# A head norm with one product and no spread, a quarter's end in another order, and one more early weight tile in a one-core fp32 block pair

## The chip, the cores and the metric

One of the eight cores of a Trainium2 chip runs the whole program. The metric is device time in microseconds (us), lower is better. The kernel before takes 2919.57 us, the median of 3 runs that lie between 2918.3 and 2920.6 us. In the text, PE is TensorE, DVE is VectorE, ACT is ScalarE, POOL is GpSimd and SP is the engine that issues most transfers.

## The reference, cut to what matters

The program computes two transformer-like blocks after one another on 1024 tokens of width 1024, in float32. The first block has a mixer with a recurrence (heads of 64 channels) and a convolutional feed-forward; the second puts 16 meta tokens in front (1040 columns), has a gated linear recurrence (8 heads, 128 keys, 64 values) beside a pooling mixer, and a feed-forward. Three places matter here: two norms per head of 64 channels, and the projection of the second block's mixer.

```
# block 1, after the recurrence: norm per head (64 channels)
mu = mean(y, -1); var = mean(square(y - mu), -1)
y = (y - mu) * rsqrt(var + GN_EPS)           # then gain, bonus, gate
# block 2, mixer
z = rmsnorm(h, norm1_g)
proj = z @ w_in                              # 1024 x 5632, 44 column blocks of 128
q, fl, iv, og, pin, ga, gb = split(proj)
S_t = diag(f_t) S_{t-1} + (1 - f_t) i_t^T ;  o_t = S_t^T q_t
o = o * rsqrt(mean(o * o, -1) + EPS)         # per head of 64 channels
o = o * head_g * silu(og)
```

## The kernel before, in words

Engines run own instruction streams that wait for each other by semaphores. Features lie on the 128 partitions and tokens along the row. A large float32 product is done as three products of a high and a low part: ACT copies a raw weight tile (128x1024) to its high part, POOL subtracts to get the low part, and PE multiplies hi by hi, hi by lo and lo by hi.

**Stages.** Three groups of stages stand behind one another, with a barrier of all engines between them (`clear_semaphores`): norm, projections and recurrence of block 1; then `middle`, with block 1's output projection, its feed-forward and block 2's mixer; then `ending`, with the branch products, block 2's output projection and feed-forward. The middle group's last instruction on any engine therefore holds up the next group on all of them.

**The recurrence's quarters** (`recurrence1`). The tokens are worked in four quarters of 256. While quarter i is prepared, the chain of the quarter before runs between. All small PE results go through a ring of two PSUM banks, `rec_e`, in the order of `quarter_pieces`: a piece may start when the piece two before it has been emptied. At the end of a quarter PE computes the score pieces `lk0` to `lk3` (emptied by DVE, `key_scores`) and the turned pieces `vt0`, `vt1`, `bt0`, `bt1` (emptied by ACT, `turns_out`), and the `var` piece, the sum of squares for the norm of the quarter before, which ACT turns into a standard deviation (`result_std`). DVE in between also forms the quarter's keys (`removal_key`, `undecayed_removal`, `undecayed_key`) and the reciprocal of that deviation (`result_inverse`).

**The join of feed-forward and mixer.** At the end of block 1's feed-forward the token tiles 0 to 7 and the 16 meta tokens pass one after another through: last product (PE), addition (DVE), statistics (ACT), scale, residual and norm (DVE), turn by 8 transposes (PE, `turn_tile`), high part (ACT), low part (DVE). `turn_tile(n)` turns token tile n-1; so `turn_tile(8)` is the last, with token tile 7. Into the gaps the mixer's first weight tile is placed: `first_dense` is piece 0 (400 columns, 24 products), `second_dense` half of piece 1, `rest_of_second` the other half.

**The mixer** (`mixer2`). Its projection has 44 blocks of three pieces (`dense`), 348, 348 and 344 columns. A piece is 24 products. All go through a ring of three PSUM banks, `mix_e`, in the order of `mixer_pieces`, mostly emptied by ACT. After the first nine blocks come 32 slots, four to a head. A slot holds three pieces and the recurrence of 256 tokens of one head: DVE builds the tree of decays for the next slot (`forget`, `double`, `whole_tiles`) and masks the scores (`mask`), PE makes `scores`, `outputs`, `keys`. After each pair of heads (8 slots) comes the norm: ACT squares the pair's output (`squares`), PE sums over each head into 16 rows (`sums_of`: 8 products of 130 columns with a `window` of ones), ACT takes the root, DVE the reciprocal of an 80x130 tile (`inverse`), PE spreads it back over the 128 rows (`spread`: 8 products with 16 rows of `expand`, in three pieces), and DVE multiplies (`finish`: two instructions per piece). For the fourth pair this falls into the mixer's tail, beside the last pieces, together with the splitting of the other branch's operand (`split_ob`, 4 rows).

Of the kernel before, what the change touches and what calls it, by code (L numbers as in the profile page):

```python
# [21 lines left out]
P = 128  # L22
# [13 lines left out]
N = 64  # L36
# [159 lines left out]
First = namedtuple("First", "first_load first_hi first_dense second_dense rest_of_second")  # L196
# [446 lines left out]
def quarter_pieces():  # L643

    order = [(n, 0) for n in ADMIT] + [("lba0", 0), ("lba1", 0)]
    for i in range(QUARTERS):
# [5 lines left out]
        order += scores[0:2] + ([("var", i - 1)] if back else []) + scores[2:]  # L652
# [24 lines left out]
def recurrence1(nc, ins, consts, table, ident, rkv, low, c, conv, projected, wout):  # L677
# [11 lines left out]
    with Scope(nc, "rec1") as s:  # L689
# [383 lines left out]
        def scalar(act):  # L1073
# [30 lines left out]
            for i in range(1, QUARTERS):  # L1104
# [7 lines left out]
                for l in range(1, LEVELS):  # L1112
# [251 lines left out]
        def vector(dve):  # L1364
# [55 lines left out]
            for i in range(1, QUARTERS):  # L1420
# [307 lines left out]
        def tensor(pe):  # L1728
# [56 lines left out]
            for i in range(1, QUARTERS):  # L1785
# [34 lines left out]
                for n, (name, b) in enumerate((("vt", 0), ("vt", 1), ("bt", 0), ("bt", 1))):  # L1820
# [4 lines left out]
                    if n < 1:  # L1825
                        level_x(5, 1, i)
                        variance(i - 1)
# [336 lines left out]
def feed_forward(nc, tag, ins, table, ident, hi, lo, f, second, post_gain, out_dst, x_src=None, gain=None, meta_src=None,  # L2164
# [39 lines left out]
    with Scope(nc, tag, at=STAGE if second else STAGE1) as s:  # L2204
# [163 lines left out]
        def sync(sp):  # L2368
# [266 lines left out]
        def tensor(pe):  # L2635
# [149 lines left out]
            following.first_dense(pe)  # L2785
            turn_tile(NT - 1)
# [16 lines left out]
        def scalar(act):  # L2803
# [462 lines left out]
BLOCKS2 = FIRST_BLOCKS + LATER_BLOCKS  # L3266
LONGER = (5, 13, 21)
# [18 lines left out]
def mixer_pieces():  # L3286

    order = []
    for n in range(len(FIRST_BLOCKS)):
        order += [("dense", 3 * n + b) for b in range(3)]  # L3290
        if 2 <= n < 6:
            order += [(f"mapped{b}", n - 2) for b in range(3)]
    for u in range(H * UNITS):
        dense = pieces_of_slot(u)
        spreads = [(f"spread{b}", u // 8 - 1) for b in range(3)] if u % 8 == 1 and u > 8 else []
        order += [("dense", dense[0])] + spreads[0:1]
        if u % 8 == 0:
            order += [(f"vt{b}", u // 8) for b in range(3)]
        order += [("kt", u), ("dense", dense[1])] + spreads[1:2]
        if u and u % 8 == 0:  # L3300
            order.append(("sum", u // 8 - 1))
        order += spreads[2:3] + [("dense", p) for p in dense[2:]]
    tail = list(range(pieces_of_slot(H * UNITS)[0], 3 * CHUNKS2))
    order += [("dense", p) for p in tail[:4]] + [("sum", PAIRS - 1)] + [("dense", p) for p in tail[4:]]
    order += [(f"spread{b}", PAIRS - 1) for b in range(3)]
# [4 lines left out]
def mixer2(nc, ins, consts, table, ident, hi, lo, proj, oa, ob, join, branch):  # L3310
# [17 lines left out]
    with Scope(nc, "mix2", at=STAGE) as s:  # L3328
# [4 lines left out]
        std, inv = (s.sb(n, [C1 + 16, GROUP]) for n in ("std", "inv"))  # L3333
# [986 lines left out]
```

## Time and profile before

| quantity | value |
|---|---|
| median of 3 runs | 2919.57 us |
| profiled execution: its own time | 2917.1 us |
| its span in the trace | 2915.0 us |
| PE busy | 2828.1 us (97% of the span) |
| DVE busy | 2001.1 us (69%) |
| POOL busy | 1122.9 us (39%) |
| ACT busy | 1013.5 us (35%) |
| granted clock of TensorE, mean | 0.994 of full |

Times in the rows below count from the start of the span. A row of the timeline gives start, duration, engine, line of the source, operation, what it writes and reads, shapes, and in brackets how long the engine was idle before it and what ended that. Ends of PE's instructions are modelled, so the distance from start to start says what a group costs. A float32 product that is not split appears as two instructions. "x6" merges six neighbours.

### The profile page before, as it was taken

The page shows a single profiled execution, that of the slowest core. Times are in us where ns is not written, and L with a number is a line of the kernel's source. Part 1 is how long each engine was busy: PE and PEld are TensorE (multiplying, and loading weights), DVE is VectorE, ACT ScalarE, POOL GpSimd, SP SyncE. Part 2 cuts the span into 40 slices and gives each one's busy share as a digit, 9 for nine tenths or more (in the row PEclk, how much of TensorE's full clock was granted, in tenths as well). Part 3 has the DMA queues.
Part 4 walks back from the last instruction along what each step waited for, and adds up shares of the span by engine and source line. Part 5 has one row for each costly group of instructions (what it writes and reads, how often), then busy time and mean ns, then how long its engine had stood idle before and what let it go on. Part 6 is the DMA issues. An engine that isn't in the chain of part 4 may idle for free. (4 is left out here: it accounts for less than half of the span.)

```text
span 2915.0 us, 55296 instructions
## 1 busy us (share of the span) xinstructions
PE 2828.1 (97%) x21636; PEld 2460.4 (84%) x21636; DVE 2001.1 (69%) x3205; ACT 1013.5 (35%) x1492; POOL 1122.9 (39%) x873
## 2 busy tenths in 40 slices
PE   7999999999999999998999999999999999999998
PEld 6787888787888888877999999999978888888887
DVE  6898865568777777777467768774436676666755
ACT  3231544434333333344223233224323333332333
POOL 0001432317656556550222232221314655555552
PEclk9999999999999999999999999999999999999999
DMA  4111000322111121124111111123421112111112
GB/s 130 46 51 37 3 3 26 107 75 63 47 53 53 47 61 47 47 81 138 44 52 57 33 52 32 51 64 112 142 85 44 51 47 61 47 54 50 47 47 87
DMA packets 205344, 173.09 MB, mean 59 GB/s; under 512 B 10573, under 2 KB 182053, under 8 KB 204773
## 3 DMA queue, kind: packets, MB, share of 16 engines
q1 hardware_dynamic: 198245, 161.88, 18.0%
q10 hardware_dynamic: 6912, 8.52, 0.8%
q8 instruction: 141, 2.31, 0.3%
q14 instruction: 46, 0.38, 0.0%
HBM read 149.27 MB, written 21.10 MB: 58 GB/s over the span
## 5 line engine op out<-in xcount | busy, mean ns | idle before, releaser
L3103 DVE TENSOR_TENSOR tokens_x<-ffn_acc,tokens_x 128x512 f32<-128x512 f32 x450 | 301.8, 686 | 66.9 <-PE ffn_acc L2659 66.7
L3920 PE MATMUL mix_e<-blk_hi,mix_w_hi 128*128 128x348 f32 (+3 forms) x1056 | 346.0, 328 | 1.8 <-DVE blk_lo L3058 1.2
L3920 PE MATMUL mix_e<-blk_lo,mix_w_hi 128*128 128x348 f32 (+3 forms) x1056 | 339.2, 321 | 0.0
L3920 PE MATMUL mix_e<-blk_hi,mix_w_lo 128*128 128x348 f32 (+3 forms) x1056 | 338.0, 320 | 0.0
L2642 PE MATMUL ffn_out<-ffn_T,ffn_w12h 128*128 128x512 f32 x1008 | 313.1, 392 | 5.6 <-POOL ffn_w12l L2520 3.5
L2659 PE MATMUL ffn_acc<-blk_hi,ffn_hid_hi 128*128 128x512 f32 x900 | 309.5, 393 | 1.3 <-issue 1.3
L3489 POOL TENSOR_TENSOR mix_w_lo<-mix_raw,mix_w_hi 128x1024 fp32r<-128x1024 f32 x44 | 109.0, 2477 | 367.1 <-ACT mix_w_hi L3524 367.1
L2520 POOL TENSOR_TENSOR ffn_w03l<-ffn_r,ffn_w03h 128x512 fp32r<-128x512 f32 x126 | 193.2, 1534 | 122.9 <-ACT ffn_w03h L2871 119.3
L2642 PEld LDWEIGHTS ffn_out<-ffn_T,ffn_w12h 128*128 128x128 f32 x1008 | 188.4, 189 | 45.8 <-POOL ffn_w12l L2520 4.4
L2520 POOL TENSOR_TENSOR ffn_w12l<-ffn_r,ffn_w12h 128x512 fp32r<-128x512 f32 x114 | 167.7, 1481 | 106.3 <-ACT ffn_w12h L2871 104.4
L3920 PEld LDWEIGHTS mix_e<-blk_hi,mix_w_hi 128*128 128x128 f32 x1056 | 198.4, 188 | 6.6 <-issue 2.0
L2659 PEld LDWEIGHTS ffn_acc<-blk_hi,ffn_hid_hi 128*128 128x128 f32 x900 | 169.1, 188 | 37.6 <-issue 1.7
L3920 PEld LDWEIGHTS mix_e<-blk_lo,mix_w_hi 128*128 128x128 f32 x1056 | 198.4, 188 | 0.3
L3920 PEld LDWEIGHTS mix_e<-blk_hi,mix_w_lo 128*128 128x128 f32 x1056 | 198.3, 188 | 0.0
L2642 PE MATMUL ffn_out<-ffn_T,ffn_w12l 128*128 128x512 f32 x504 | 197.4, 392 | 0.0
L2659 PE MATMUL ffn_acc<-blk_hi,ffn_hid_lo 128*128 128x512 f32 x450 | 175.5, 390 | 0.0
L608 DVE SCALAR_TENSOR_TENSOR mixed_conv<-in_c,top_table,mixed_conv 128x1024 f32<-128x1024 f32 x120 | 155.9, 1299 | 3.8
L2871 ACT ACTIVATE ffn_w12h<-ffn_r 128x512 fp32r<-128x512 f32 x124 | 75.3, 624 | 206.9 <-PE ffn_out L2642 196.9
L2642 PE MATMUL ffn_out<-blk_hi,ffn_w03h 128*128 128x258 f32 (+1 forms) x504 | 134.4, 321 | 4.1 <-POOL ffn_w03l L2520 2.6
L2520 POOL TENSOR_TENSOR ffn_w12l<-ffn_S,ffn_w12h 128x512 fp32r<-128x512 f32 x42 | 57.0, 1356 | 202.1 <-ACT ffn_w12h L2871 202.1
L2642 PE MATMUL ffn_out<-blk_lo,ffn_w03h 128*128 128x258 f32 (+1 forms) x504 | 133.7, 319 | 0.0
L2642 PE MATMUL ffn_out<-blk_hi,ffn_w03l 128*128 128x258 f32 (+1 forms) x504 | 133.2, 319 | 0.0
(538 smaller groups left out, 7024.1 us busy)
## 6 DMA issues: line engine op xcount, KB each, us to landing
ffn_r<-ffn_up SPq DMA_DIRECT2D x88, 256.0 KB, 3.0
mix_raw<-w_in SPq DMA_DIRECT2D x44, 512.0 KB, 3.8
ffn_r<-w_up SPq DMA_DIRECT2D x88, 256.0 KB, 3.0
ffn_room<-ffn_down SPq DMA_DIRECT2D x20, 512.0 KB, 4.0
ffn_room<-w_down SPq DMA_DIRECT2D x20, 512.0 KB, 4.0
proj_w_raw<-w_in_first SPq DMA_DIRECT2D x19, 512.0 KB, 3.8
branch_gates<-proj SPq DMA_DIRECT2D x16, 520.0 KB, 4.7
wout_raw<-w_out SPq DMA_DIRECT2D x16, 512.0 KB, 3.9
```

The source lines that it names most:

```text
L608: nc.vector.scalar_tensor_tensor(conv[:, f, :], c[:, f, t:t + T], table[:, column:column + 1], conv[:, f, :], ALU.mult, ALU.add).then_inc( ...
L2520: G.by(tt(slots[slot_][1], raw, slots[slot_][0], ALU.subtract), f"lo_{name}")
L2642: mm = nc.tensor.matmul(o, a[:, k, :], rhs, start=fresh and k == 0 and part == 0, stop=k == half - 1 and part == 2, skip_group_check=True)
L2659: mm = nc.tensor.matmul(accs[t % len(accs)], a[:, par, i * P:(i + 1) * P], b[:, h, :], start=part == 0, stop=part == 2)
L2871: A.by(activation(slots[slot_][0], raw, ACT.Copy), f"hi_{name}")
L3103: return vec.tensor_tensor(dst, accs[t % len(accs)], dst, ALU.add)
L3489: tt(w_lo[n % 2][:], raw[:], w_hi[n % 2][:], ALU.subtract).then_inc(lo_ready, 1)
L3920: last = nc.tensor.matmul(dst[:, 0:m], a[n % 2][:, kd, :], b[:, kd, c:c + m], start=kd == 0 and part_ == 0, stop=kd == KD - 1 and part_ == 2)
```

## The change

**Recurrence.** In each of the quarters 1 to 3 the `var` piece moves from third to fifth place in the ring's order, behind `lk1` and `vt1`. ACT empties `vt0` and `vt1` before it takes the deviation. DVE empties `lk0` and then `lk1` before the quarter's keys are formed; the keys' instructions are the same.

PE at the end of quarter 1, before (`rec_e` are the ring's pieces: `rec_center` is in the vt pieces, `rec_head_window` in var, `top_ident` in bt, 64x128 in lk):

```order
L1571 MATMUL rec_lv<-rec_xt,rec_tt 64x64 x16
L1507 MATMUL rec_e<-rec_sqd,rec_head_window 16x128 x8
L1538 MATMUL rec_e<-rec_ar_109,mixed_rkv 64x128 x8
L1549 MATMUL rec_e<-rec_center,mixed_rkv 64x64 x16
L1538 MATMUL rec_e<-rec_ar_109,mixed_rkv 64x128 x8
```

The same place on PE after the change:

```order
L1569 MATMUL rec_lv<-rec_xt,rec_tt 64x64 x16
L1536 MATMUL rec_e<-rec_ar_109,mixed_rkv 64x128 x8
L1547 MATMUL rec_e<-rec_center,mixed_rkv 64x64 x16
L1505 MATMUL rec_e<-rec_sqd,rec_head_window 16x128 x8
L1536 MATMUL rec_e<-rec_ar_109,mixed_rkv 64x128 x8
```

The var piece has moved behind the second lk and the second vt piece.

**Feed-forward's end.** The mixer's second weight tile is loaded (SP, with token tile 3), split in its high part (ACT, after the statistics of token tile 5) and its low part (POOL, as soon as that is there), and piece 3 (348 columns of it) is computed right behind piece 0. The ring's order begins 0, 3, 1, 2. The second tile's buffers lie at other addresses.

PE at the feed-forward's end, before (`mix_e` are the mixer's products, `ffn_out<-top_ident` the turn of token tile 6):

```order
L3920 MATMUL mix_e<-blk_hi,mix_w_lo_7104 128x400
L2747 MATMUL ffn_out<-top_ident,ffn_y 128x128 x8
L3920 MATMUL mix_e<-blk_hi,mix_w_hi_7102 128x384
L3920 MATMUL mix_e<-blk_lo,mix_w_hi_7102 128x384
L3920 MATMUL mix_e<-blk_hi,mix_w_lo_7104 128x384
```

After the change, with the first three and the last three of the 24 new rows of 348 columns:

```order
L3927 MATMUL mix_e<-blk_hi,mix_w_lo_7103 128x400
L3927 MATMUL mix_e<-blk_hi,mix_w_hi_7102 128x348
L3927 MATMUL mix_e<-blk_lo,mix_w_hi_7102 128x348
L3927 MATMUL mix_e<-blk_hi,mix_w_lo_7100 128x348
...
L3927 MATMUL mix_e<-blk_hi,mix_w_hi_7102 128x348
L3927 MATMUL mix_e<-blk_lo,mix_w_hi_7102 128x348
L3927 MATMUL mix_e<-blk_hi,mix_w_lo_7100 128x348
L2748 MATMUL ffn_out<-top_ident,ffn_y 128x128 x8
```

The turn of token tile 6 now stands behind those 24 products; they are gone from their place behind piece 2.

**Head norm of the mixer.** `head_ones` (128x128, ones within each head) takes the place of the window: one product per piece gives the sum already on all rows of the head. ACT takes the root of three pieces (128x348, 128x348, 128x344) into `factor`, DVE takes the reciprocal of those (in place) and multiplies from there. The products with `expand` are gone, and so are two small loads. For the first three pairs `inverse` and `finish` of a piece stand at the ends of slots 1, 2 and 3 of the next pair; for the last pair all three follow the four `split_ob` rows.

DVE in the mixer's tail, before:

```order
L3829 TENSOR_TENSOR branch_oblo<-mixed_ob,branch_obhi 128x1040 x2
L3813 RECIPROCAL mix_inv<-mix_std 80x130
L3829 TENSOR_TENSOR branch_oblo<-mixed_ob,branch_obhi 128x1040 x2
L3820 SCALAR_TENSOR_TENSOR mix_o<-mix_e,top_table,mix_o 128x390
L3823 TENSOR_TENSOR mixed_oa<-mix_o,mixed_oa 128x390
L3820 SCALAR_TENSOR_TENSOR mix_o<-mix_e,top_table,mix_o 128x390
L3823 TENSOR_TENSOR mixed_oa<-mix_o,mixed_oa 128x390
L3820 SCALAR_TENSOR_TENSOR mix_o<-mix_e,top_table,mix_o 128x260
L3823 TENSOR_TENSOR mixed_oa<-mix_o,mixed_oa 128x260
```

And after:

```order
L3843 TENSOR_TENSOR branch_oblo<-mixed_ob,branch_obhi 128x1040 x4
L3826 RECIPROCAL mix_factor<-mix_factor 128x348
L3834 SCALAR_TENSOR_TENSOR mix_o<-mix_factor,top_table,mix_o 128x348
L3837 TENSOR_TENSOR mixed_oa<-mix_o,mixed_oa 128x348
L3826 RECIPROCAL mix_factor<-mix_factor 128x348
L3834 SCALAR_TENSOR_TENSOR mix_o<-mix_factor,top_table,mix_o 128x348
L3837 TENSOR_TENSOR mixed_oa<-mix_o,mixed_oa 128x348
L3826 RECIPROCAL mix_factor<-mix_factor 128x344
L3834 SCALAR_TENSOR_TENSOR mix_o<-mix_factor,top_table,mix_o 128x344
L3837 TENSOR_TENSOR mixed_oa<-mix_o,mixed_oa 128x344
```

The one small reciprocal between the rows of `split_ob` has become three large ones behind them. The diff, cut:

```
@@ quarter_pieces
-        order += scores[0:2] + ([("var", i - 1)] if back else []) + scores[2:]
+        order += scores[0:4] + ([("var", i - 1)] if back else []) + scores[4:]
@@ recurrence1: scalar
+                turns_out(i, ("vt",))
                 result_std(i - 1)
-                turns_out(i, ("vt", "bt"))
-                turns_out(i, ("kt",))
+                turns_out(i, ("bt", "kt"))
@@ recurrence1: vector
+                key_scores(0, i)
                 last_level(0, i)
-                key_scores(0, i)
                 last_level(1, i)
-                if more:
-                    removal_key(i + 1)
                 key_scores(1, i)
                 if more:
-                    undecayed_removal(i + 1)
+                    removal(i + 1)
                     undecayed_key(i + 1)
                 result_inverse(i - 1)
@@ feed_forward: sync, tensor, scalar
+                if i == 3:
+                    following.second_load(sp)
...
             following.first_dense(pe)
+            following.next_dense(pe)
             turn_tile(NT - 1)
...
                 tile_statistics(i)
+                if i == 5:
+                    following.second_hi(act)
@@ mixer2
+EARLY_PIECES = (0, 3, 1, 2)
...
-            def deviation(j):
+            def deviation(j, b):
...
+                activation(factor[:, c:c + m], bank(f"sum{b}", j)[:, 0:m], ACT.Sqrt, scale=1.0 / N, bias=eps[:])
...
-                vec.reciprocal(inv[:], std[:]).then_inc(inv_ready, 1)
+                vec.reciprocal(factor[:, c:c + m], factor[:, c:c + m]).then_inc(inv_ready, 1)
...
-                vec.scalar_tensor_tensor(o[:, j % 2, cs], bank(f"spread{b}", j)[:, 0:cs.stop - cs.start], hg, o[:, j % 2, cs],
-                                         ALU.mult, ALU.mult).then_inc(taken(f"spread{b}", j), 1)
+                vec.scalar_tensor_tensor(o[:, j % 2, cs], factor[:, cs], hg, o[:, j % 2, cs], ALU.mult, ALU.mult)
...
-                if u and u % 8 == 0:
-                    inverse(u // 8 - 1)
+                if u > 8 and 1 <= u % 8 <= 3:
+                    inverse(u // 8 - 1, u % 8 - 1)
+                    finish(u // 8 - 1, u % 8 - 1)
...
-            inverse(PAIRS - 1)
             for row in range(2, 4):
                 split_ob(row)
             for b in range(3):
+                inverse(PAIRS - 1, b)
                 finish(PAIRS - 1, b)
@@ mixer2: tensor
+            def head_sums(j, b):
+                c, m = THIRDS[b]
+                pe.wait_ge(squared, j + 1)
+                dst = start_piece(pe, f"sum{b}", j)
+                end_piece(mm(dst[:, 0:m], head_ones[:], sf[:, 1, c:c + m], start=True, stop=True), f"sum{b}", j)
...
                 scores(u, tiles[1])
                 if u and u % 8 == 0:
-                    sums_of(u // 8 - 1)
+                    head_sums(u // 8 - 1, 0)
                 outputs(u, tiles[0])
-                if spreading:
-                    spread(u // 8 - 1, 2)
+                if u and u % 8 == 0:
+                    head_sums(u // 8 - 1, 1)
                 dense(pieces[2])
+                if u and u % 8 == 0:
+                    head_sums(u // 8 - 1, 2)
```

## Rows read from the trace of the kernel before

**Rows 1.** The page, busy time, share of the span and instructions of each engine

```profile
PE 2828.1 (97%) x21636; PEld 2460.4 (84%) x21636; DVE 2001.1 (69%) x3205; ACT 1013.5 (35%) x1492; POOL 1122.9 (39%) x873
```

**Rows 2.** Waits of PE: us in total, times, longest us

```profile
PE ffn_out L2747 <- DVE ffn_y L3052: 3.3, 1, 3.3
PE rec_e L1538 <- DVE rec_lk L1270: 3.3, 2, 1.7
...
PE rec_e L1538 <- ACT rec_vt L993: 2.9, 2, 1.5
...
PE rec_e L1538 <- ACT mixed_rkv L993: 1.4, 1, 1.4
...
PE mix_e L3920 <- DVE blk_lo L3058: 1.2, 1, 1.2
```

**Rows 3.** Timeline of quarter 1's end, by engine: ACT, PE, DVE

```profile
379.66 1.28 ACT L1012 ACT_TABLE_LOAD   x1
...
385.51 1.09 PE L1538 MATMUL rec_e<-rec_ar,mixed_rkv 64*64 64x128 f32 x16 [1.45 <-ACT rec_vt L993]
...
391.06 1.09 PE L1538 MATMUL rec_e<-rec_ar,mixed_rkv 64*64 64x128 f32 x16 [1.65 <-DVE rec_lk L1270]
...
386.64 0.69 DVE L1270 TENSOR_TENSOR rec_lk<-rec_e,rec_both 128x512 f32<-128x512 f32 x1 [1.71 <-PE rec_e L1538]
...
390.38 0.63 DVE L1270 TENSOR_TENSOR rec_lk<-rec_e,rec_both 128x512 f32<-128x512 f32 x1
```

**Rows 4.** Timeline of the mixer's begin, PE: pool products, then a dense piece

```profile
1390.45 1.91 PE L3944 MATMUL mix_e<-mix_work,mix_w_pool 128*128 128x348 f32 x6
...
1392.35 0.32 PE L3920 MATMUL mix_e<-blk_lo,mix_w_hi 128*128 128x348 f32 x1
1392.51 0.32 PE L3920 MATMUL mix_e<-blk_hi,mix_w_lo 128*128 128x348 f32 x1
```

**Rows 5.** Timeline of the feed-forward's end, DVE and PE

```profile
1345.38 1.28 DVE L3052 SCALAR_TENSOR_TENSOR ffn_y<-tokens_x,ffn_inv,ffn_gains 128x1024 f32<-128x1024 f32 x1
...
1347.02 1.28 DVE L3038 SCALAR_TENSOR_TENSOR tokens_x<-tokens_x,ffn_inv,ffn_post_gains 128x1024 f32<-128x1024 f32 x1
...
1361.24 0.98 PE L2747 MATMUL ffn_out<-top_ident,ffn_y 128*128 128x128 f32 x7 [3.31 <-DVE ffn_y L3052]
```

**Rows 6.** Timeline in a slot, POOL and DVE at one moment

```profile
1645.57 2.40 POOL L3489 TENSOR_TENSOR mix_w_lo<-mix_raw,mix_w_hi 128x1024 fp32r<-128x1024 f32 x1 [10.18 <-ACT mix_w_hi L3524]
...
1645.64 2.49 DVE L3747 TENSOR_TENSOR mix_work<-mix_work,mix_sf 128x128 f32<-128x128 f32 x1
```

**Rows 7.** Timeline of slots 8 and 9, PE: sums, and a spread piece

```profile
1605.59 1.29 PE L4035 MATMUL mix_e<-mix_sf,mix_window 128*16 128x130 f32 x16
1606.81 0.32 PE L4010 MATMUL mix_out<-mix_work,mix_vt 128*64 128x128 f32 x1
...
1615.07 0.93 PE L4045 MATMUL mix_e<-mix_inv,mix_expand 16*128 16x130 f32 x6
1615.93 0.32 PE L4010 MATMUL mix_out<-mix_work,mix_vt 128*64 128x128 f32 x1
```

**Rows 8.** Groups by form, DVE reciprocals: count, busy us, mean ns, idle before

```profile
L3813 DVE RECIPROCAL mix_inv<-mix_std 80x130 f32<-80x130 f32 x4 | 3.8, 956 | 2.4 <-ACT mix_std L3630 2.4
...
L3843 DVE RECIPROCAL mix_lower<-mix_lower 128x8 f32<-128x8 f32 x1 | 0.2, 203 | 0.0
```

**Rows 9.** Busy us (instructions) in one slot without norm: PE, PEld, DVE, ACT, POOL

```profile
1633.41:1648.57 15.16, 15.16 (x158) 14.62 (x154) 12.21 (x43) 7.89 (x11) 4.51 (x9) 1.00 0.13 37
```

**Rows 10.** Timeline of the mixer's tail and the next group, DVE and PE

```profile
2005.77 3.74 DVE L3829 TENSOR_TENSOR branch_oblo<-mixed_ob,branch_obhi 128x1040 fp32r<-128x1040 f32 x2 [1.09 <-ACT branch_obhi L3639]
...
2012.94 0.48 DVE L3820 SCALAR_TENSOR_TENSOR mix_o<-mix_e,top_table,mix_o 128x260 f32<-128x260 f32 x1
2013.45 0.43 DVE L3823 TENSOR_TENSOR mixed_oa<-mix_o,mixed_oa 128x260 f32<-128x260 f32 x1
...
2015.45 0.92 PE L4167 MATMUL branch_out<-branch_obhi,branch_w_hi 128*128 128x348 f32 x2 [4.44 <-PEq L191]
```

More of the change, by code:

```diff
@@ L3286, in mixer_pieces @@
 def mixer_pieces():
-    order = []
+    order = [("dense", p) for p in EARLY_PIECES]
     for n in range(len(FIRST_BLOCKS)):
-        order += [("dense", 3 * n + b) for b in range(3)]
+        order += [("dense", p) for p in range(3 * n, 3 * n + 3) if p not in EARLY_PIECES]
         if 2 <= n < 6:
@@ L3294, in mixer_pieces @@
         dense = pieces_of_slot(u)
-        spreads = [(f"spread{b}", u // 8 - 1) for b in range(3)] if u % 8 == 1 and u > 8 else []
-        order += [("dense", dense[0])] + spreads[0:1]
+        sums = [(f"sum{b}", u // 8 - 1) for b in range(3)] if u and u % 8 == 0 else []
+        order.append(("dense", dense[0]))
         if u % 8 == 0:
             order += [(f"vt{b}", u // 8) for b in range(3)]
-        order += [("kt", u), ("dense", dense[1])] + spreads[1:2]
-        if u and u % 8 == 0:
-            order.append(("sum", u // 8 - 1))
-        order += spreads[2:3] + [("dense", p) for p in dense[2:]]
+        order += [("kt", u), ("dense", dense[1])] + sums[0:2] + [("dense", dense[2])] + sums[2:3]
+        order += [("dense", p) for p in dense[3:]]
     tail = list(range(pieces_of_slot(H * UNITS)[0], 3 * CHUNKS2))
-    order += [("dense", p) for p in tail[:4]] + [("sum", PAIRS - 1)] + [("dense", p) for p in tail[4:]]
-    order += [(f"spread{b}", PAIRS - 1) for b in range(3)]
+    order += [("dense", p) for p in tail[:4]] + [(f"sum{b}", PAIRS - 1) for b in range(2)]
+    order += [("dense", tail[4]), ("sum2", PAIRS - 1)] + [("dense", p) for p in tail[5:]]
     assert sum(name == "dense" for name, _ in order) == 3 * CHUNKS2 and sorted(BLOCKS2) == list(range(CHUNKS2))
@@ L3639, in split_ob @@
                 activation(branch.ob[0][:, k, :], ob[:, k, :], ACT.Copy).then_inc(ob_hi_ready, 1)
-            for p in range(3):
+            for p in EARLY_PIECES:
                 evacuate(p)
@@ L3646, in scalar @@
             act.wait_ge(join.stored, 16 * NT)
-            for p in range(3, 18):
+            for p in range(4, 18):
                 evacuate(p)
@@ L3667, in scalar @@
                 activations(u)
-                for p in dense[2:]:
+                evacuate(dense[2])
+                if u and u % 8 == 0:
+                    deviation(u // 8 - 1, 2)
+                for p in dense[3:]:
                     evacuate(p)
@@ L3677, in scalar @@
             evacuate(tail_pieces[3])
-            deviation(PAIRS - 1)
+            deviation(PAIRS - 1, 0)
+            deviation(PAIRS - 1, 1)
             branch_weight()
@@ L3681, in scalar @@
             split_ob(3)
-            for p in tail_pieces[4:]:
+            evacuate(tail_pieces[4])
+            deviation(PAIRS - 1, 2)
+            for p in tail_pieces[5:]:
                 evacuate(p)
@@ L3870, in vector @@
                     double(u + 1, 0)
-                if spreading:
-                    finish(u // 8 - 1, 0)
                 if u:
@@ L4052, in tensor @@
             for n in range(1, len(FIRST_BLOCKS)):
-                for b in range(3):
-                    dense(3 * n + b)
+                for p in range(3 * n, 3 * n + 3):
+                    if p not in EARLY_PIECES:
+                        dense(p)
                 if 2 <= n < 6:
                     mapped(n - 2)
-            pe.wait_ge(consts_landed, 96)
+            pe.wait_ge(consts_landed, 80)
             for u in range(slots):
                 pieces, tiles, earlier = pieces_of_slot(u), tiles_of(u), before(u)
-                spreading = u % 8 == 1 and u > 8
                 dense(pieces[0])
-                if spreading:
-                    spread(u // 8 - 1, 0)
                 if u:
```

109 lines of the change are left out of this document (48 added, 61 removed).

## The prediction

> **What bounds the kernel now.** I read the page's busy shares first: PE is busy for 97% of the span, so its idle time in all is 87 us [rows 1]. A change can gain in two ways, by taking work from PE or by closing one of its gaps, and it can lose wherever another engine comes to hold PE. So the second view is the list of what PE waited for. The places of this change stand there with 3.3, 2.9 and 1.4 us (the score pieces of the recurrence's quarters, which wait for DVE and ACT) and 3.3 and 1.2 us (the feed-forward's end, which waits for DVE) [rows 2]. In the mixer's slots PE hardly waits: in one slot it is busy for all of 15.16 us, with DVE at 12.21 [rows 9]. There only PE's own work counts, as long as DVE stays below it. The one place where another engine ends last is the mixer's tail: DVE's last multiplication starts at 2013.45 and takes 0.43, and PE begins the next group at 2015.45 after 4.44 us without work, behind the barrier [rows 10].
>
> **Recurrence, three quarters.** Now PE waits 1.45 us at 385.51 because ACT sat in the deviation, behind var, before it emptied vt0, and 1.65 us at 391.06 because DVE empties lk2 only at 390.38 + 0.63 [rows 3]. With the new order lk1 needs lk0's bank, which DVE empties early, so lk1 starts where var does now, and vt1, var and lk2 follow without a gap. The first wait goes. The second is set by DVE: it had 1.71 us idle before it emptied lk1 at 386.64 [rows 3], between the key instruction and that. Now lk1 is emptied before the keys, so the same row of instructions (three of the keys, one reciprocal, lk2) runs through without that hole. It saves what the hole was less what DVE waits for lk1 at its new place. lk1 now starts at about 382.9, is emptied at 384.0 to 384.7, keys and reciprocal take DVE to 389.0, lk2's emptying to 389.7: lk3 starts at 389.7 where it was 391.06, 1.4 us earlier. ACT loads its root table (1.28 us [rows 3]) later than before, behind vt1, which delays bt0 by under 1 us, but bt0 ends before 389.7. Quarter 2 has the same waits (each count in rows 2 is 2). In quarter 3 DVE has no keys to form, so only the 1.4 us wait stood there; there the table load decides: root at 1.3 us behind vt1's emptying, then the reciprocal, then lk2, which brings lk3 to within 0.1 us of where it was. Term: 1.4 + 1.4 + 0.1 = 2.9 us gained. Bounds: nothing if DVE's chain is as late as now, 7.6 us if all waits of rows 2 at these pieces go.
>
> **Feed-forward's end.** Piece 3 is 24 products at 0.16 us from start to start (1392.35 to 1392.51 [rows 4]), 3.8 us. It now fills PE's holes of 1.2 and 3.3 us [rows 2] and leaves its old place, where PE had no hole. It delays the turn of token tile 6, whose high part ACT only takes later anyway, behind tile 7's statistics. So the whole 3.8 us would be gained if the last turn at 1361.24 stays. It does not. POOL's subtraction for this tile (2.40 us [rows 6]) used to run after the last turn; now it falls at about 1345.6, when ACT has made the high part. DVE is then in the two-input instruction that runs from 1345.38 to 1346.66 [rows 5]. Rows 6 show what comes of that: a DVE instruction of 128 columns that began while POOL subtracted took 2.49 us, to POOL's end. So POOL starts at 1346.6, ends near 1348.9, and DVE's next one, at 1347.02 [rows 5], ends 1.9 us late; the high part on ACT (1.05 us) hides in that. DVE's chain to the last turn has no slack, for PE waits 3.31 us for it [rows 5]. Term: 3.8 - 1.9 = 1.9 us gained. Bounds: 1.4 (a full 2.4 lost) and 3.8 (none).
> The Trainium skill (SBUF — State Buffer, section on the two separate sides) says that DVE with two SBUF inputs and GpSimd take a shared port pair by an exclusive lock, for the whole instruction. The trace agrees [rows 6]; it is why I put the loss near POOL's whole duration.
>
> **PE's work in the norm.** Removed per pair: sums 1606.81 - 1605.59 = 1.22 us; two spread pieces of three products at 1615.93 - 1615.07 = 0.86, and one of two at two thirds, 0.57: 3.51 us [rows 7]. Added: three float32 products of the form of the pooling product (128*128, 348 columns): three of them, six instructions, ran from 1390.45 to 0.16 before 1392.35, 1.74 us [rows 4]. So 1.77 us per pair, and for the three pairs within the slots 5.3 us gained. Two small loads less are off any path. Bounds: 4 to 6.
>
> **DVE's work in the norm.** The reciprocal costs 956 ns at 130 columns and 203 at 8 [rows 8], 6.2 ns a column; at 348 it is 2.3 us. The multiplications cost 0.48 and 0.43 at 260 columns [rows 10] and 1.28 at 1024 [rows 5], so 0.57 and 0.52 at 348. A block is 3.4 us. In slots 9 to 11 of a pair DVE gets 3.4 us each, where it now has 1 us in one slot and some 3.2 in the next. 12.21 + 3.4 is 15.6 against PE's 15.16 [rows 9]: just over, for three slots in a row (12.21 holds one stall behind POOL of the kind in rows 6). DVE runs ahead of PE by a few us, which covers most. I take 0.5 us of PE waits per pair, 1.5 us lost. Bounds: 0, and 2.4 + 0.45 in each of nine slots, 25.7, if the new two-input instructions meet POOL's subtraction a second time.
>
> **The tail.** Here nothing covers DVE. The four split rows end at 2009.51 now [rows 10]; the roots of the first two pieces hold ACT about 0.2 longer, so they end near 2009.7. Then come three blocks of 3.4, to 2019.9, where DVE now ends at 2013.88 [rows 10]. The barrier follows, and PE behind it, at the same distance of 1.6 us. PE's own end (no spreads, 1.74 for 1.22 in sums) is 2010 either way, the last store lands earlier than 2019.9. Term: 6.0 us lost. Bounds: 0.3 if a large reciprocal cost only as much as a multiplication, 8.
> The Trainium skill (VectorE: DVE Perf Modes, section on the fixed hardware budget) says that Reciprocal runs as an iterated division with a repeat count of 8. An estimate from that at 8 cycles of 0.96 GHz is 8.3 ns a column, 2.9 us for 348; the tail would lose 7.9 and the sum would be 0.7 us gained. The rows have 6.2 ns, up to 130 columns; they decide.
>
> **Sum.** -2.9 - 1.9 - 5.3 + 1.5 + 6.0 = -2.6 us. The profiled execution took 2917.1 (span 2915.0 and 2.1 around it), so it would take 2914.5; the median of the runs lies 2.5 us above it, so 2917.0.
>
> **Rivals.**
> A, the covers hold: POOL's subtraction misses DVE's chain (1.9 back) and the slots take the reciprocals whole (1.5 back): -6.0, 2913.6. For it: PE waits for nothing in the slots now, and DVE idles 2.95 us in the slot shown. Against: rows 6, and 15.6 over 15.16. Chance 0.18.
> B, slower: DVE becomes the bound in slots 9, 10 and 11 of three pairs. Each finish brings two two-input instructions into a stretch where POOL subtracts for 2.4 us; if each slot's block meets it, DVE needs 12.21 + 3.4 + 2.4 = 18.0 us against 15.16, 2.85 us in nine slots, and with the rest (-4.1) the kernel takes +21.6: 2941. It decides from 1.1 us a slot (9.9 in all) for more than 0.2% lost; halfway, 2928. For it: DVE's new share. Against: the stall behind POOL is one per slot, whichever instruction meets it, and is in the 12.21. Chance 0.10.
> C, the large reciprocal is much cheaper than its columns say: the tail loses 0.3 only, the slots nothing: -9.8, 2909.8. Against: rows 8. Chance 0.05.
> D, the recurrence gives nothing, since the new wait (lk1 on lk0, var on lk1, both emptied by DVE) takes the place of the old: +0.3, 2919.9. For it: each piece now hangs on DVE twice. Against: DVE's 1.71 us hole. Chance 0.12.
> The forecast itself has 0.55, with its own range of 2914.5 to 2919.5.
>
> **Numbers.** What three runs can tell from no change is about 0.2%, 5.8 us: faster means below 2913.7, slower above 2925.4. Faster: half of A, C and the low edge of the forecast, 0.20. Slower: most of B and a little of the rest, 0.10. Same: 0.70. The range leaves out C and the upper B: 2912.5 to 2923.
>
> **What would show it.** In the profile after: (1) quarters 1 and 2: no wait for rec_vt, lk3 about 1.4 us earlier against the lk0 before it; (2) piece 3 between the turns, a stretched DVE instruction near 1347, the last turn some 1.9 us later than 1361.24 against token tile 0's; (3) 24 instructions with head_ones at 0.29 us; reciprocals of 2.3 us; (4) waits of PE in slots 9 to 12 of 1 to 2 us in sum; (5) DVE's end some 10 us behind PE's last product, and a wait of PE at the barrier of about 11 us where it was 4.44. The forecast is wrong if (5) is under 8 us or (4) over 6.

## The result, and the profile after

The changed kernel takes 2926.97 us (median of 6 runs, 2921.25 to 2930.2) where the one before takes 2918.94 (6 runs, 2917.29 to 2921.22): 1.0029 of it, 95% interval 1.0019 to 1.0039. It is 8 us slower. The forecast was 2917.0, with a range that ended at 2923. The profiled execution's span is 2922.0 us against 2915.0; its own time, 2923.98 us, lies 3 us under the median of the six and 9.5 above the 2914.5 that the forecast had for it.

First the list of what PE waited for, of the whole program after the change (us in total, times, longest). It answers to [rows 2] and, in its first line, to the wait of [rows 10]:

```profile
PE branch_out L4164 <- PEq L191: 11.5, 1, 11.5
PE mix_out L4015 <- DVE mix_S L3818: 5.8, 3, 2.8
...
PE ffn_out L2748 <- DVE ffn_y L3056: 3.1, 2, 2.8
...
PE mix_out L4020 <- DVE mix_work L3808: 2.3, 3, 0.9
PE rec_e L1536 <- DVE rec_lk L1270: 2.2, 3, 0.9
PE rec_e L1547 <- ACT rec_y_std L1012: 2.1, 3, 0.7
```

The second and fourth lines are new: in the mixer's slots, where PE waited for nothing but 0.9 us of turned values, it now waits 8.1 us for DVE. `mix_S` is the state that goes from one tile of tokens to the next, `mix_work` under L3808 the masked scores. The waits of 5.8 us stand at slots 12, 20 and 28, one in each of the first three pairs' norms: 2.31, 2.81 and 0.68 us.

The second view cuts PE's time at four instructions that both programs have: the mixer's first product, the feed-forward's last turn, the first sums of the tail, and the first product of the next group. Each number below is the distance of two such starts in one profiled execution:

| stretch | before | after | forecast for the change |
|---|---|---|---|
| start to mixer's first product | 1348.78 | 1345.41 | -2.9 |
| to the feed-forward's last turn | 12.46 | 14.21 | +1.9 |
| to the tail's sums (first nine blocks and all slots) | 639.41 | 643.32 | -3.8 (piece) - 5.3 + 1.5 |
| to the next group's first product | 14.80 | 21.04 | +6.0 |
| to the end | 899.55 | 898.02 | 0 |

The second and fourth lines came out near the forecast, and the last is no part of the change. The first did too, but single profiles scatter by more than its 3.4 us there (last section), so it proves nothing by itself. The third stretch, called "the slots" below, was to be 7.6 us shorter and is 3.9 longer: an error of 11.5 us, which is the whole miss.

Third, the moment of the longest kind of wait, slot 11 to 12 (DVE, then PE; start, duration, engine, line, operation). L3826, L3834 and L3837 are the third block of the pair, L3793 with 16x80 is the mask of the head's last 16 tokens:

```profile
1652.14 2.30 DVE L3826 RECIPROCAL mix_factor<-mix_factor 128x344 f32<-128x344 f32 x1
1654.55 2.02 DVE L3834 SCALAR_TENSOR_TENSOR mix_o<-mix_factor,top_table,mix_o 128x344 f32<-128x344 f32 x1
1656.60 0.52 DVE L3837 TENSOR_TENSOR mixed_oa<-mix_o,mixed_oa 128x344 f32<-128x344 f32 x1
1657.03 0.22 DVE L3793 TENSOR_TENSOR mix_work<-mix_sc,mix_masks 16x80 f32<-16x80 f32 x1
...
1660.10 0.27 DVE L3818 SCALAR_TENSOR_TENSOR mix_S<-mix_S,mix_work,mix_upd 128x64 f32<-128x64 f32 x1
```

```profile
1652.20 0.21 PE L3992 MATMUL mix_sc<-mix_q,mix_work 128*16 128x16 f32 x2
...
1660.51 0.25 PE L4015 MATMUL mix_out<-mix_work,mix_vt 16*64 16x16 f32 x2 [2.31 <-DVE mix_S L3818]
```

The scores are there at 1652.20, but DVE is in the block until 1657.03, and PE's product with the new state starts 0.41 us behind the state update. The same place before the change:

```profile
1659.16 0.21 PE L3982 MATMUL mix_sc<-mix_q,mix_work 128*16 128x16 f32 x2
...
1665.30 0.25 PE L4005 MATMUL mix_out<-mix_work,mix_vt 16*64 16x16 f32 x2
```

```profile
1659.61 0.23 DVE L3778 TENSOR_TENSOR mix_work<-mix_sc,mix_masks 16x80 f32<-16x80 f32 x1 [1.47 <-PE mix_sc L3982]
...
1664.89 0.27 DVE L3803 SCALAR_TENSOR_TENSOR mix_S<-mix_S,mix_work,mix_upd 128x64 f32<-128x64 f32 x1
```

PE's product stood 0.41 us behind the update there too (1664.89 and 1665.30), with no wait shown. DVE had no lead at all at this point. From scores to state it took 5.73 us before and 7.90 after: 2.17 more, and PE's wait is 2.31.

At slot 12 the block's first multiplication (2.02 us) also met POOL's subtraction. At slot 20, the place of the longest wait, it did not and took 0.57:

```profile
1788.76 2.29 DVE L3826 RECIPROCAL mix_factor<-mix_factor 128x344 f32<-128x344 f32 x1
1791.16 0.57 DVE L3834 SCALAR_TENSOR_TENSOR mix_o<-mix_factor,top_table,mix_o 128x344 f32<-128x344 f32 x1
...
1795.26 0.27 DVE L3818 SCALAR_TENSOR_TENSOR mix_S<-mix_S,mix_work,mix_upd 128x64 f32<-128x64 f32 x1
```

```profile
1786.87 0.21 PE L3992 MATMUL mix_sc<-mix_q,mix_work 128*16 128x16 f32 x2
...
1795.67 0.36 PE L4015 MATMUL mix_out<-mix_work,mix_vt 16*64 16x16 f32 x2 [2.81 <-DVE mix_S L3818]
```

Before the change PE's product stood 0.80 us behind the update at slots 20 and 28, so there 0.39 us were to spare. From scores to state it took 5.13 us at slot 20 and takes 8.39 now, 3.26 more; at slot 28 it took 5.16 and takes 6.29, 1.13 more. Less the 0.39 that is 2.9 and 0.7; the waits are 2.81 and 0.68.

Last, what PE ran at behind two such waits (stretch, length, PE busy and instructions, granted clock as a share of full speed, DMA):

```profile
1659.00:1662.00 3.00, 1.49 (x12) 1.00 0.11 33
1662.00:1665.00 3.00, 3.00 (x12) 0.50 0.00 0
1665.00:1668.00 3.00, 3.00 (x47) 0.93 0.00 0
1793.00:1796.00 3.00, 0.33 (x3) 0.85 0.00 0
1796.00:1799.00 3.00, 3.00 (x13) 0.50 0.00 0
1799.00:1802.00 3.00, 3.00 (x13) 0.51 0.00 0
```

The waits of 2.31 and 2.81 us are each followed by a stretch at 0.50, the lower of the two levels (1.2 GHz instead of 2.4). By the shares of these rows PE lost 1.7 us in the first (3 x 0.50 + 3 x 0.07) and 3.0 in the second. The distances say a little less: from the product behind the wait to the next pair's turned values (L3970) PE took 67.93 and 69.32 us where it took 66.45 and 66.52 before the change, so 1.5 and 2.8 us. The waits of 0.9 us and less in the slots were followed by no such stretch.

### The profile page after: what moved, and what is told of

Same layout as the page of the kernel before. It is cut to its first block and busy times, and to the rows that moved or that the text cites. A ratio compares the mean times of both kernels' runs of the same rounds, so it can differ in the third digit from the quotient of the medians.

```text
span 2922.0 us, 55097 instructions
## 1 busy us (share of the span) xinstructions
PE 2827.1 (97%) x21532; PEld 2458.0 (84%) x21532; DVE 2027.0 (69%) x3212; ACT 1016.0 (35%) x1496; POOL 1123.1 (38%) x873
```

## The experiments

Each was timed in five rounds beside the kernel before, except the last. A ratio is to the kernel before, with its 95% interval. A number of us "under the changed kernel" compares medians of different sets of runs: the kernel before had 2918.94 us beside the changed kernel and 2918.59, 2917.93 and 2916.49 beside the experiments, so taken against it these numbers are 0.4 to 1.0 us smaller. The edits are cut to the lines that matter ("..." marks a cut). Line numbers of an experiment's rows are those of its own source.

**Recurrence alone.** Only the new order of the ring's pieces, with DVE's and ACT's order to match.

```diff
-        order += scores[0:2] + ([("var", i - 1)] if back else []) + scores[2:]
+        order += scores[0:4] + ([("var", i - 1)] if back else []) + scores[4:]
...
```

> The kernel before with the recurrence's new order alone. Theory one (the two traces): its quarters save 1.2 and 1.5 us, the third about nothing, so 2.7 us less than before (0.9991 of it). The rest of the shift seen ahead of the feed-forward (1.07 us at the start, 1.5 us near 331 us) is not of this edit and does not come back. Rival: the new waits of each score piece on DVE take the gain back over several executions, 0 +- 0.5 us.

Measured 0.9992 (0.9983 to 1.0000), medians 2916.34 and 2918.59: 2.3 us faster, near the theory; the interval just reaches to no gain, so the time alone doesn't rule the rival out. In its trace the quarters take 10.48, 10.48 and 9.95 us from lk0 to lk3 where they took 11.88, 11.88 and 10.09.

**Head norm alone.** The changed kernel with the recurrence's and the feed-forward's end undone.

```diff
-EARLY_PIECES = (0, 3, 1, 2)
+EARLY_PIECES = (0, 1, 2)
...
-        order += scores[0:4] + ([("var", i - 1)] if back else []) + scores[4:]
+        order += scores[0:2] + ([("var", i - 1)] if back else []) + scores[2:]
```

> The changed kernel with the recurrence's old order and the feed-forward's end as before: the head norm alone is new. Theory one: the norm alone costs all of the loss and more: 2927.0 + 2.7 (recurrence) + 2.0 (early piece, 3.8 less the 1.75 by which the last turn is later) = 2931.7, so 12.7 us over before (1.0044). Rival: the early piece or the moved order disturbs the mixer's slots, and without them the norm costs under 6 us (below 1.002).

Measured 1.0041 (1.0027 to 1.0055), 2930.18 against 2918.59: 11.6 us slower where 12.7 was expected. In its trace the slots take 648.27 us, of which 3.8 are the piece that is back in them, so 644.5 where the changed kernel has 643.3 (this profile has a stretch at the lower clock behind the last turn, worth about 1 us, which the changed kernel's has not; see "Old norm, the rest new"), and PE's waits there are the same 5.8 and 2.2. The norm alone makes the loss, and the other two parts don't touch it.

**Third block later.** The third block at the end of slot 5 of a pair, not 3.

```diff
+NORM_SLOTS = (1, 2, 5)
...
-                if u > 8 and 1 <= u % 8 <= 3:
-                    inverse(u // 8 - 1, u % 8 - 1)
-                    finish(u // 8 - 1, u % 8 - 1)
+                if u > 8 and u % 8 in NORM_SLOTS:
+                    inverse(u // 8 - 1, NORM_SLOTS.index(u % 8))
+                    finish(u // 8 - 1, NORM_SLOTS.index(u % 8))
```

> The changed kernel with the third of a pair's three blocks (reciprocal and two multiplications on DVE) moved from the end of slot 11 to the end of slot 13 of its pair (slots 3 and 5 of the eight), the first two left. Theory one, placement: in slot 3 the block stands in front of the state update for the head's last 16 tokens, on which PE waits 2.3, 2.8 and 0.7 us and after two of which PE runs at half its clock; moved, these waits go and the clock stays at 1.00: 7 to 10 us less than the changed kernel, 2917 to 2920. Theory two, throughput and the lock behind POOL: a slot with 12.2 us of DVE work has no room for 3.4 us more wherever it stands; the waits turn up in slot 5 instead and the time stays within 2 us of the changed kernel.

Measured 0.9998 (0.9990 to 1.0007), 2917.72 against 2918.59: 9.2 us under the changed kernel. The wait for `mix_S` is gone from the list, and the slots take 634.76 where they took 643.32. The state update of slot 12 and PE's product in this kernel (DVE, PE):

```profile
1653.26 0.23 DVE L3794 TENSOR_TENSOR mix_work<-mix_sc,mix_masks 16x80 f32<-16x80 f32 x1 [0.43 <-PE mix_sc L3993]
...
1658.53 0.27 DVE L3819 SCALAR_TENSOR_TENSOR mix_S<-mix_S,mix_work,mix_upd 128x64 f32<-128x64 f32 x1
```

```profile
1652.81 0.21 PE L3993 MATMUL mix_sc<-mix_q,mix_work 128*16 128x16 f32 x2
...
1658.95 0.25 PE L4016 MATMUL mix_out<-mix_work,mix_vt 16*64 16x16 f32 x2
```

From scores to state it is 5.72 us again, as before the change. DVE's work in the slots is the same as in the changed kernel, so theory two (a slot has no room for the block wherever it stands) falls.

**Third block without its reciprocal.** Left in slot 3, with the deviation itself multiplied in; the reciprocal of this third of the columns is left out for three pairs.

```diff
-                    inverse(u // 8 - 1, u % 8 - 1)
+                    if u % 8 < 3:
+                        inverse(u // 8 - 1, u % 8 - 1)
...
```

> The changed kernel with the reciprocal of each first three pairs' third block left out (the deviation itself is multiplied in), the two multiplications left in slot 3: the block is 1.1 us where it was 3.4. Theory one (what counts is how long DVE is kept from the state update in slot 3): the waits for that update fall from 2.3, 2.8 and 0.7 to 0, 0.5 and 0, the clock no longer falls, and the time is 8 to 10 us under the changed kernel, 2917 to 2919, as with the block moved away. Rival (the two-input multiplications meet POOL's subtraction, and that stretch is the loss): they are all still there, and no more than 3 us come back.

Measured 1.0003 (0.9994 to 1.0012), 2919.06 against 2917.93: 7.9 us under the changed kernel. The slots take 635.21 us. The waits for the state fell from 5.8 to 1.1 us in all, and slot 12's is the last of these lines (the first two are DVE's, ahead of it):

```profile
1655.97 0.57 DVE L3834 SCALAR_TENSOR_TENSOR mix_o<-mix_factor,top_table,mix_o 128x344 f32<-128x344 f32 x1
...
1657.68 2.37 DVE L3808 TENSOR_TENSOR mix_work<-mix_work 16x16 f32<-16x16 f32 x1
```

```profile
1662.70 0.25 PE L4018 MATMUL mix_out<-mix_work,mix_vt 16*64 16x16 f32 x2 [0.67 <-DVE mix_S L3818]
```

The multiplications and POOL's subtraction are all still there, but at slot 12 they no longer meet: the block's first multiplication takes 0.57 us where it took 2.02, and POOL's stretch falls on an instruction behind the mask (2.37), still between scores and state. So this run alone doesn't part the two theories at slot 12; 2.3 us less in front of the update are 1.64 less to wait. Slots 20 and 28 do. There the block met POOL in neither kernel (0.57 or 0.58 each time), and the waits fell from 2.81 and 0.68 to 0.42 and nothing. Meeting POOL is not what costs, the length in front of the state update is. No stretch at the lower clock is left in the slots beyond the one behind the last turn.

**Third block behind the update.** In slot 4, right after the state update.

```diff
                     state(u - 1, before(u)[1])
+                if u > 8 and u % 8 == 4:
+                    inverse(u // 8 - 1, 2)
+                    finish(u // 8 - 1, 2)
                 if more:
                     double(u + 1, 1)
...
-                if u > 8 and 1 <= u % 8 <= 3:
+                if u > 8 and 1 <= u % 8 <= 2:
```

> The changed kernel with the third block not at the end of slot 3 but in slot 4, right behind the state update for which PE waits. Theory one (order alone counts): the waits for the state are gone, the block now stands in front of level products and the next mask, which PE needs some 3 us later; 6 to 10 us under the changed kernel. Rival (slots 3 and 4 have no room at all): a wait for the mask takes its place, 2 to 3 us in each pair, and no more than 3 us come back.

Measured 1.0011 (1.0002 to 1.0020), 2921.24 against 2917.93: 5.7 us under the changed kernel, a little under what theory one asked. Its list of waits in the slots:

```profile
PE mix_out L4023 <- DVE mix_work L3808: 5.3, 6, 1.5
```

No wait for the state is left, but those for score masks went from 2.3 to 5.3. The slots take 638.16, between 634.76 and 643.32. The rival was half right: PE paces itself on DVE at more than one place of a slot.

**Old norm for the last pair.** Window sums, small reciprocal and spread products for the last pair only.

```diff
-            for row in range(2, 4):
-                split_ob(row)
-            for b in range(3):
-                inverse(PAIRS - 1, b)
-                finish(PAIRS - 1, b)
+            last_inverse()
+            for row in range(2, 4):
+                split_ob(row)
+            for b in range(3):
+                last_finish(b)
...
```

> The changed kernel with the last pair's norm in the old form (sums by a window, a small reciprocal, spread products), the other three pairs in the new form. Theory one: the wait at the barrier falls from 11.5 to about 4.4 us, but PE does 1.8 us more ahead of it, of which all lies in DVE's shadow: DVE ends 8 us earlier, 2919 (8 us less than the changed kernel). Rival: the last store or ACT holds the barrier next, and only 3 to 5 us come back.

Measured 1.0009 (1.0000 to 1.0019), 2921.49 against 2918.59: 5.5 us under the changed kernel, where I had expected 8. The wait at the barrier did fall as expected:

```profile
PE branch_out L4218 <- PEq L191: 4.4, 1, 4.4
```

The expectation had DVE's end 8 us earlier. It is 6.2 earlier, counted from the sums: PE waits 7.1 us less, but reaches the barrier 0.9 later with the old products. The stretch from sums to next group is the measure: 14.81 us against 21.04, 6.2 less, which is the forecast's 6.0.

**Later block and old tail together.** Both edits above.

> The changed kernel with both edits: the third block moved from slot 3 to slot 5 of a pair, and the last pair's norm in the old form. If the two gains lie in different places they add: 9.2 us from the block and 5.5 from the tail, so 2912.2, 6.4 us under before (0.9978). If the slots only hand their delay on to the tail, less than 11 us come back: 2916 or more.

Measured 0.9988 (0.9979 to 0.9997), 2914.36 against 2917.93, so 12.6 us under the changed kernel where the sum of the two was 14.7; expected was 2912.2. The gains add within what the runs can tell; its trace has 633.92 and 14.82 us for the two stretches.

**Old norm, the rest new.** The kernel before with the recurrence's order and the early weight tile.

```diff
-        order += [("dense", 3 * n + b) for b in range(3)]
+        order += [("dense", p) for p in range(3 * n, 3 * n + 3) if p not in EARLY_PIECES]
...
```

> The kernel before with the recurrence's order and the early weight tile, and the head norm all in the old form. Theory: 2.3 us from the recurrence and 2.0 from the early piece: 2914.3 (0.9985). Against the run with later block and old tail it shows what the new norm is worth in the slots once it waits for nothing: three pairs of 1.77 us less PE work, minus what waits remain (2.5 us): 2 to 3 us in favour of the new norm. Rival for the early piece: POOL's lock eats its whole gain, 2916.3.

Measured 0.9976 (0.9966 to 0.9986), 2910.0 against 2917.93: 7.9 us faster where 4.3 was expected, and faster than the run above, against the traces. So both were run again.

> The old norm with recurrence order and early piece, again, beside the run above: the two edits' gain by the traces is 2.5 + 2.0 us, 2914; the first time it measured 7.9 under before. If that was the draw of the executions, 2912 to 2915; if the early piece is worth more than its trace shows, 2909 to 2911 again.

Measured 0.9983 (0.9974 to 0.9992), 2911.76 against 2916.49: 4.7 us.

> Later block and old tail, again, on the same chip as the old norm with the rest new: their traces had the slots' stretch at 633.9 and 636.5 us, so this one should be 2.6 us faster, but the medians stood at 2914.4 and 2910.0. If the traces tell it, the order of the two turns round or they lie within 2 us; if the new norm costs outside the stretch that a single trace shows, this one is again 3 to 5 us slower.

Measured 0.9990 (0.9981 to 0.9999), 2912.88 against 2916.49: 3.6 us. The two lie 1.1 us apart: they can't be told apart by these times, though their traces have 634.9 and 636.5 us in the slots.

The two profiles of "later block and old tail" are of one kernel, and their slots differ by 0.98 us (633.92 and 634.90). In the second the granted clock is 0.50 for 3 us behind the last turn, in the first it is 1.00 there; PE had waited 2.80 us ahead of that turn in both. Of the ten profiles with a wait of 2.76 to 2.80 us at this place six have such a stretch; the changed kernel's, the old tail's and the halved blocks' have none.

**Blocks halved.** Later block and old tail, with reciprocals and multiplications in different slots.

```diff
+INVERSES, FINISHES = (0, 2, 5), (1, 4, 6)
...
-                if u > 8 and u % 8 in NORM_SLOTS:
-                    inverse(u // 8 - 1, NORM_SLOTS.index(u % 8))
-                    finish(u // 8 - 1, NORM_SLOTS.index(u % 8))
+                if u >= 8 and u % 8 in INVERSES:
+                    inverse(u // 8 - 1, INVERSES.index(u % 8))
+                if u >= 8 and u % 8 in FINISHES:
+                    finish(u // 8 - 1, FINISHES.index(u % 8))
```

> The kernel with later block and old tail, but each block of the slots cut in two: reciprocals at the ends of slots 0, 2 and 5 of a pair, the two multiplications at the ends of slots 1, 4 and 6. DVE's work is the same, the longest stretch before other work is 2.3 us where it was 3.4. Theory (what PE waits for is the length that stands in front of a score mask or state update): the 2.6 us of waits for masks that are left there fall under 1 us, the slots' stretch from the last turn to the tail's sums falls from 633.9 to about 632, and the time is 1 to 3 us less. Rival (DVE's sum in the slots is what PE waits for): the waits stay at 2.6.

Measured 0.9970 (0.9959 to 0.9981), 2909.26 against 2916.49: 7.2 us faster than before. That is the lowest ratio of all, though its interval overlaps those of the old norm with the rest new. Against whole blocks in the run beside it (2912.88) it is 3.6 us, where 1 to 3 were expected. The slots take 630.36 us, 4.5 less than in that run's profile and 3.6 less than in the other profile of that kernel, which like this one has no stretch at the lower clock behind the last turn; the waits that went are 2.6. Of PE's waits in the mixer and at its tail only these are left:

```profile
PE branch_out L4220 <- PEq L191: 4.4, 1, 4.4
PE ffn_out L2748 <- DVE ffn_y L3056: 2.8, 1, 2.8
PE mix_e L4006 <- ACT mix_vt L3629: 1.1, 4, 0.4
PE mix_e L3963 <- issue: 0.3, 1, 0.3
```

DVE does all of the new norm's work in the slots, and PE waits for none of it.

**Low part of the early weight late.** The old norm with the rest new; POOL's subtraction for the early tile waits for the feed-forward's last split, and the early piece leaves out its eight products with the low part.

```diff
                 pool.wait_ge(hi_ready, n + 1)
+                if n == 1:
+                    pool.wait_ge(join.lo_ready, NT + 1)
...
```

> The kernel with old norm and the rest new, with POOL's subtraction for the early weight tile held back until the feed-forward's last split is done, and the early piece without its eight products with the low part (left out). One look at the trace. Theory: the 1.75 us by which the last turn came later against the mixer's first product (14.21 where it was 12.46) is POOL's lock on DVE alone, so it is back at 12.4 to 12.6 and DVE's multiplication takes 1.28 us where it took 2.93. Rival: ACT's extra high part (1.05 us) delays the statistics too, and 13.2 or more is left.

It ran once (2910.89 us), for its trace. From it, the instruction that the changed kernel stretches (first fence, from the changed kernel, with POOL's beside it) and the same in this kernel (second fence):

```profile
1342.22 3.38 POOL L3495 TENSOR_TENSOR mix_w_lo<-mix_raw,mix_w_hi 128x1024 fp32r<-128x1024 f32 x1 [36.76 <-ACT mix_w_hi L3530]
...
1343.74 2.93 DVE L3042 SCALAR_TENSOR_TENSOR tokens_x<-tokens_x,ffn_inv,ffn_post_gains 128x1024 f32<-128x1024 f32 x1
```

```profile
1343.32 1.29 DVE L3042 SCALAR_TENSOR_TENSOR tokens_x<-tokens_x,ffn_inv,ffn_post_gains 128x1024 f32<-128x1024 f32 x1
```

The last turn comes 12.54 us behind the mixer's first product, where the changed kernel has 14.21 and the one before 12.46. POOL's subtraction is nearly all of the 1.75 us; ACT's extra instruction costs less than 0.1.

## Why the prediction was wrong

**Recurrence (forecast -2.9): right.** From lk0, the piece behind lbr, to lk3 the new order takes 10.64, 10.48 and 9.95 us in quarters 1 to 3 where it took 11.88, 11.88 and 10.09: 1.24, 1.40 and 0.14 less, against 1.4, 1.4 and 0.1. The run of this edit alone measured 2.3, with an interval that reaches to nothing. New waits did come: PE waits 0.91 us for lk in quarters 1 and 2, as the forecast said of DVE's chain, and 0.71 us for ACT's deviation in each quarter, ahead of bt0, where it had "under 1 us".

**Feed-forward's end (forecast -1.9): right, and for the reason given.** The piece of 3.8 us left the stretch of the slots, the last turn is 1.75 us later against the mixer's first product. The Trainium skill (SBUF — State Buffer, on the two separate sides) has DVE with two SBUF inputs and GpSimd exclude each other for whole instructions; the trace agrees (the last experiment: 2.93 us with POOL at work, 1.29 without).

**PE's work in the norm (forecast -5.3): right, and visible only where nothing waits.** With halved blocks the slots take 630.36 us, with the old norm 636.5: 6.1 less. The 0.8 above the forecast is about the 0.98 us of the stretch at the lower clock that follows the last turn in the second kernel's profiles and not in the first's. This rests on the traces: the runs of the two lie 2.5 us apart (2909.26 and 2911.76), and their intervals overlap.

**The tail (forecast +6.0): right.** Measured 6.2 in the traces and 5.5 between the runs. The reciprocal of 348 columns took 2.32 us, as worked out from the rows. The Trainium skill (VectorE: DVE Perf Modes, on the fixed hardware budget) gives a repeat count of 8, from which the estimate was 2.9; the measurement decides.

**DVE's lag in the slots (forecast +1.5): this step failed.** It measured 13.0: the slots are 3.9 us longer, and the piece (3.8) and PE's work (5.3) that left them come on top. The changed kernel against halved blocks says the same, 643.3 less 630.4, and all of it lies in the three pairs with a norm: 4.0, 6.6 and 2.4 us. Two things stood behind the 1.5. The first was a comparison of sums: 15.6 us of work in a slot of 15.16, so half a microsecond short. The second was the sentence "DVE runs ahead of PE by a few us, which covers most". The idle time of DVE was taken for a lead. It was none: DVE idles because it waits for PE's scores, and once it has them, PE waits for the state that comes out of them. At slot 12 that chain, scores to state, takes 5.73 us, and PE started 0.41 us behind the update already before the change, which is what it takes when it waits; at slots 20 and 28 it had 0.39 us to spare. Of a block of 3.4 us put in front of slot 12's mask only what DVE idled there before, 1.47 us, is free, which leaves 1.9. The rest is paid: the block kept DVE until 4.83 us behind the scores, POOL's stretch inside it, and the chain came to 7.90, 2.17 more.

Second, the price of a wait was taken as its length. 8.1 us of waits for DVE cost 12.4 of the 13.0, because two of them were followed by stretches at the lower clock (1.5 + 2.8 us by the distances above). The sum had no term for the clock at all.

Rival B had the place (slots 9 to 11), the sign and, at its halfway point of 2928, nearly the time, but not the mechanism. It too added work and stall per slot. The stall behind POOL is there once a slot in any case, as the forecast held against it: in the slots' stretch 30 DVE instructions took over 0.4 us more than the median of their form, 56 us in all, before the change, and 30, 57 us, after it; with halved blocks, where the time is lowest, they are 33 and 63 us. What decides is where in the slot the block stands, which the runs with the third block moved and slots 20 and 28 of the one without its reciprocal show. That B's time came near is luck. The chance of 0.10 for it, and 0.10 for slower, was too small for a case whose check, the slack at the places where PE takes something from DVE, had not been made.

Of the other rivals, A fell on both its covers (1.75 us at the feed-forward's end, 13.0 in the slots), C on the 2.32 us of the reciprocal, D on the quarters' 2.8 us. The signs named beforehand told it at once: (1), (2), (3) and (5) stood as described, the last with 11.5 us at the barrier; (4), waits of 1 to 2 us in sum in slots 9 to 12, stood at 8.1, over the 6 from which the forecast was to be wrong.

## What to carry to other kernels

Before work is added to an engine that seems to have room, follow each thing it hands to the bottleneck back to what releases it, and compare the time from release to hand-over with the time until it is needed; idle time that ends on the bottleneck's own signal is part of a loop, and is not a lead. Put added work where it stands in front of nothing that is waited for, and in short pieces: the same DVE work in the slots cost 13 us in one order and nothing in another. And price a wait of PE with what its clock does behind it.

## What the runs showed of the hardware

In the slots PE's granted clock was 0.50 for the products that followed waits of 2.31 and 2.81 us, in all three profiles that have these waits (the changed kernel, head norm alone, old tail), and did not fall behind waits of 0.9 us and less, nor behind one of 1.53 (third block behind the update). Behind the first that cost 1.5 us more, behind the other 2.8. A wait's length alone does not tell: behind one of 2.8 us ahead of the last turn the clock fell in six profiles of ten (in one of the two profiles of later block and old tail, and not in the other), and behind one of 3.3 at the same place it did not fall before the change and did with the head norm alone.

While POOL's subtraction and a two-input DVE instruction met, either could be the one that was late. In the slot of [rows 6] DVE took 2.49 us to POOL's 2.40. In the feed-forward's end POOL took 3.38 us and DVE 2.93 (1.29 alone): there both lost. DVE instructions with one tensor as input were held too: before the change one of 128x256 (L3730, at 1660.81) took 2.50 us beside POOL's 2.41, where the same at 1792.89 took 0.29.

A single trace is not enough for a part of 3 us in every place. The first stretch, up to the mixer's first product, which is nearly the same program in all kernels with the new recurrence, lay between 1343.61 and 1349.13 us in their twelve profiles. The stretch from sums to next group (14.80 to 14.82, or 21.03 to 21.04) repeats to a few hundredths. The slots repeat to 0.2 us where the clock does the same (636.49 and 636.51, 643.32 and 643.45) and differ by 0.98 where it does not.
